# Gate, up and first-matrix products: low products of one half issued in turn with high products of the other half

## Chip, core and metric

The kernel runs on one core of a Trainium2 chip. The metric is device time in microseconds. A row of the profile can name several engines: PE is the matmul engine (TensorE), PEld its loads of the stationary operand, DVE the vector engine, ACT the scalar engine, POOL GpSimd, SP the engine that issues DMAs. TensorE's clock has two levels, 1.2 and 2.4 GHz; its granted share is 1.00 in the stretches shown here, which is 2.4 GHz.

## What is computed

Three transformer layers over 256 tokens of width 1024, in float32: a mixer of a bidirectional mLSTM and a spatial gating unit, a latent attention, and a chunked attention with a relative bias. Each has a feed-forward part behind it:

```python
x = x + jnp.square(jax.nn.relu(hf @ ffn_w1[layer])) @ ffn_w2[layer]      # layers 0 and 1, 1024 -> 4096 -> 1024
x = x + rms_norm_2(swiglu(h, w_gate, w_up, w_down), g_post_ffn)          # last layer, 1024 -> 2816 -> 1024
def swiglu(h, w_gate, w_up, w_down):
    return (jax.nn.silu(h @ w_gate) * (h @ w_up)) @ w_down
```

The products whose order is changed are `hf @ ffn_w1` (the first matrix of a feed-forward part), `h @ w_gate` and `h @ w_up`.

## The kernel before

Every weight comes from memory in pieces of 128 partitions by 2048 numbers (1 MB), in a ring of three slots. ScalarE rounds a piece to the matmul's reduced float32 (`w_hi`), and VectorE makes the rest, `w_lo = raw - w_hi`. The activations are split in the same way, into `h_hi` and `h_lo`, which lie side by side in `h_both`. A product is then a sum of three terms, high x high, high x low and low x high. The fourth is left out.

A piece of a first matrix has 256 output columns, in two halves of 128 (f = 0 and 1), and eight blocks of 128 input rows (k = 0 to 7). The function `stationary_both` (L2083) works one such piece. Half f has a PSUM bank of its own, `b + f`, with 512 columns of float32.

- A *high* product (L2090) has the block of `w_hi` as the stationary operand and streams 512 columns of `h_both`, that is `h_hi` and `h_lo` of the 256 tokens. The high x high terms end in columns 0 to 255 of the bank and the high x low terms in columns 256 to 511.
- A *low* product (L2096) has the block of `w_lo` as the stationary operand, streams the 256 columns of `h_hi` and adds to columns 0 to 255 of the same bank.

Each half needs eight highs and eight lows. Each of the 32 matmuls of a call has its own stationary operand. The order before is: eight highs of half 0, eight highs of half 1, eight lows of half 0, eight lows of half 1. When the last low has ended, `piece_used` is raised. DVE waits for it and adds the two 256-column parts of both banks in one reduction (L1608 in the first two feed-forward parts, L1925 and the one of `glu_mul` in the last). ScalarE waits for it before it writes the slot of the ring again.

Ahead of a call, PE waits with `split` until the `w_lo` of the piece is ready, and for the reduction that last read the two banks (`hid_in`, `gate_scaled` or `mul_out`).

The call stands in two loops. In `ffn` (L2423), which runs for two layers, the first piece has a function of its own, and each of the 15 further chunks is one call, followed by `out_piece` (L2176), the second matrix of the chunk before: 24 matmuls of 512 columns (L1984, L1985, L1986 in turn). In the last stage `gate_up` (L2855) makes one call for the gate and one for the up piece of each of ten chunks, and `out_piece` follows. Its very last call passes `half_done`: there half 0 is finished first (highs, lows) and then half 1, so that VectorE can begin with half 0.

Three other places are of use in reading the trace. `stationary_half` (L2070) does one half at a time, eight highs (L2076) and eight lows (L2079), in the projection of queries and keys of the last layer. `latent_in` (L2469) streams 384 and 288 columns in turn into two banks, and its low terms (L2048) alternate singly between the two sizes. `turn_x` (L2000) transposes blocks of 128 x 128 (L2005).

Of the kernel before, what the change touches and what calls it, by code (L numbers as in the profile page):

```python
# [34 lines left out]
P = 128  # L35
D = 1024
KB = D // P
S = 256
# [97 lines left out]
def build(nc, d, out):  # L136

    ctx = ExitStack()
    with ctx:
        def sb(name, shape, dt=F32):  # L140
            return ctx.enter_context(nc.sbuf_tensor(name, shape, dt))

        def sem(name):
            return ctx.enter_context(nc.semaphore(name))
# [9 lines left out]
        h_both = sb("h_both", [P, KB, 2, S], F32R)  # L154
        h_hi, h_lo = h_both[:, :, 0, :], h_both[:, :, 1, :]
# [144 lines left out]
        piece_used = sem("piece_used")  # L300
# [152 lines left out]
        def part(t, n, a):  # L453

            w = width(n)
            return t[:, n % RING, 0:w].rearrange("p (a b) -> p a b", a=a)
# [26 lines left out]
        def bank(b, n=1):  # L483
            return psum[:, b:b + n, :].rearrange("p b c -> p (b c)")
# [1496 lines left out]
        def _(pe):  # L1981
            def product(dst, stat, mov, first, last, shared=False):

                pe.matmul(dst, stat[0], mov[0], start=first, stop=False, skip_group_check=shared)  # L1984
                pe.matmul(dst, stat[0], mov[1], start=False, stop=False, skip_group_check=shared)  # L1985
                return pe.matmul(dst, stat[1], mov[0], start=False, stop=last, skip_group_check=shared)  # L1986

            def h_block(k, tb=None, t=None):
                if tb is None:
                    return h_hi[:, k, :], h_lo[:, k, :]  # L1990
                if t == T_2MIX:
                    return [mix_part(t, k // 2, a, b)[:, k % 2, tb * P:(tb + 1) * P]
                            for a, b in ((h_hi, g_hi), (h_lo, g_lo))]
                return h_hi[:, k, tb * P:(tb + 1) * P], h_lo[:, k, tb * P:(tb + 1) * P]
# [88 lines left out]
            def stationary_both(slot, b, half_done=None):  # L2083


                wh = w_hi[:, slot, :].rearrange("p (k c) -> p k c", k=KB)
                wl = w_lo[:, slot, :].rearrange("p (k c) -> p k c", k=KB)
                def high(f):
                    for k in range(KB):
                        pe.matmul(bank(b + f), wh[:, k, f * P:(f + 1) * P],  # L2090
                                  h_both[:, k, :, :].rearrange("p u s -> p (u s)"),
                                  start=k == 0, stop=False, skip_group_check=True)

                def low(f):
                    for k in range(KB):
                        ins = pe.matmul(bank(b + f)[:, 0:S], wl[:, k, f * P:(f + 1) * P], h_hi[:, k, :],  # L2096
                                        start=False, stop=k == KB - 1, skip_group_check=True)
                    return ins

                high(0)  # L2100
                if half_done is not None:
                    low(0).then_inc(half_done, 1)
                    high(1)
                else:
                    high(1)
                    low(0)
                low(1).then_inc(piece_used, 1)

            def stationary_seam(slot, t, b, x_at):

# [179 lines left out]
            for k in range(KB):  # L2290
                ins = product(bank(7)[0:3 * QUAD + A_H, 0:S],
                              (gw_hi[:, k, 0:3 * QUAD + A_H], gw_lo[:, k, 0:3 * QUAD + A_H]), h_block(k),
                              k == 0, k == KB - 1)
# [10 lines left out]
            wh = w_hi[:, 1, :].rearrange("p (k c) -> p k c", k=KB)  # L2304
            wl = w_lo[:, 1, :].rearrange("p (k c) -> p k c", k=KB)
            pe.wait_ge(hi_half, 2)
            for f in range(2):
                for k in range(KB):
                    at = bank(QK_ORDER[1])[:, f * S:(f + 1) * S]
                    pe.matmul(at, wh[:, k, f * P:(f + 1) * P], h_hi[:, k, :], start=f == 0 and k == 0, stop=False,  # L2310
                              skip_group_check=True)
                    pe.matmul(at, wh[:, k, f * P:(f + 1) * P], h_lo[:, k, :], start=False, stop=False,
                              skip_group_check=True)
# [3 lines left out]
            for f in range(2):  # L2317
                for k in range(KB):
                    ins = pe.matmul(bank(QK_ORDER[1])[:, f * S:(f + 1) * S], wl[:, k, f * P:(f + 1) * P], h_hi[:, k, :],
                                    start=False, stop=k == KB - 1, skip_group_check=True)  # L2320
# [10 lines left out]
            for q, rows in enumerate((a_row, mt_row)):  # L2331
                for tb in range(TB):
                    at = (2 * q + tb) * ROWS
                    ins = pe.transpose(bank(6)[:, at:at + ROWS], rows[0:ROWS, tb * P:(tb + 1) * P],
                                       ident[0:ROWS, 0:ROWS])
# [87 lines left out]
            def ffn(first, hb, t, x_at, x_next):  # L2423
                split(first)
                stationary_seam(first % RING, t, 0, x_at)

                def chunk(c, j, i):

                    n = first + 1 + 2 * j
                    split(n + 12 * i)  # L2430
                    if not (isinstance(c, int) and c == 0):
                        pe.wait_ge(hid_in, hb + c)
                    stationary_both(n % RING, hidden_banks(j + 1))
                    split(n + 1 + 12 * i)
                    pe.wait_ge(g_lo_ready, hb + c + 1)
                    out_piece(hidden_of(j % 3), (n + 1) % RING, isinstance(c, int) and c == 0)

                def hidden_of(r):
                    return lambda k, tb: (g_hi[:, r, k * S + tb * P:k * S + (tb + 1) * P],
                                          g_lo[:, r, k * S + tb * P:k * S + (tb + 1) * P])  # L2440

                for j in range(3):
                    chunk(j, j, 0)
                with pe.Fori(0, (FC - 4) // 6) as i:
                    for j in range(3, 9):
                        chunk(6 * i + j, j, i)
                n = first + 2 * FC - 1
                split(n)
                pe.wait_ge(g_lo_ready, hb + FC)
                out_seam(hidden_of((FC - 1) % 3), n % RING, x_next)  # L2450
# [55 lines left out]
            for j in range(3):  # L2506
                n = P_UQ + j
                split(n)
                wh, wl = part(w_hi, n, 3), part(w_lo, n, 3)
                if j:  # L2510
                    pe.wait_ge(latent_read, j)
                for tb in range(TB):
                    if j == 1 and tb == 1:
# [4 lines left out]
                        for t in range(TB):  # L2518
                            ins = pe.transpose(psum[0:C_QK, 4, t * P:(t + 1) * P], krr[:, t, :], ident[:, :])
                        ins.then_inc(krr_turned, 1)  # L2520
                    for k in range(3):
                        if j == 0 and tb == 0 and k == 2:
                            turn_latent(1, 0, 3)
                        if j == 0 and k < 2:
                            latent_wait(2 * tb + k)
                        ins = product(bank(UQ_BANKS[j] + tb), h_block(k, tb), (wh[:, k, :], wl[:, k, :]),
                                      k == 0, k == 2)
# [18 lines left out]
            def c_values(j, tb):  # L2546

                wh, wl = part(w_hi, P_UKV + j, 2), part(w_lo, P_UKV + j, 2)
                for k in range(2):
                    ins = product(bank((0, 4)[j] + tb), h_block(3 + k, tb), (wh[:, k, 512:], wl[:, k, 512:]),  # L2550
                                  k == 0, k == 1)
                return ins
# [3 lines left out]
            for j in range(2):  # L2556
                n = P_UKV + j
                split(n)
                wh, wl = part(w_hi, n, 2), part(w_lo, n, 2)
                pe.wait_ge(evac_q, 2 + j)  # L2560

                for pair in range(4):
                    hs = slice(pair * P, (pair + 1) * P)
                    for k in range(2):
                        ins = product(bank((6, 2)[j], 2)[:, pair * S:(pair + 1) * S],
                                      (wh[:, k, hs], wl[:, k, hs]), h_block(3 + k), k == 0, k == 1)
# [7 lines left out]
                if j == 0:  # L2574
                    for tb in range(TB):
                        ins = c_values(0, tb)
# [278 lines left out]
            def gate_up(c, r, n0, i):  # L2855
                split(n0 + 6 * i)
                if not (isinstance(c, int) and c == 1):
                    pe.wait_ge(gate_scaled, c)
                stationary_both(n0 % RING, 4)
                split(n0 + 1 + 6 * i)  # L2860
                pe.wait_ge(mul_out, hb + c)
                stationary_both((n0 + 1) % RING, 6, up_half if isinstance(c, int) and c == GC - 1 else None)
# [53 lines left out]
```

## Time and profile before

| | us |
|---|---|
| median of three runs (873.94 to 874.26) | 874.14 |
| the profiled execution | 874.67 |
| its span, from the first to the last instruction | 872.9 |
| PE busy | 864.1 (99%) |
| PEld busy | 739.8 (85%) |
| DVE busy | 622.4 (71%) |
| ACT busy | 452.9 (52%) |

The profile is of one execution. Busy times of PE overlap, since a matmul begins before the one ahead of it has ended, so the mean duration of a matmul is longer than the distance from one to the next. The distances stand in the chain of waits, which shares the time out among the instructions that followed each other, and in the starts of a timeline. Both are given to 0.01 us. A run of the same line is merged into one row with its count.

### The profile page before, as it was taken

The page shows a single profiled execution, that of the slowest core. Times are in us where ns is not written, and L with a number is a line of the kernel's source. Part 1 is how long each engine was busy: PE and PEld are TensorE (multiplying, and loading weights), DVE is VectorE, ACT ScalarE, POOL GpSimd, SP SyncE. Part 2 cuts the span into 40 slices and gives each one's busy share as a digit, 9 for nine tenths or more (in the row PEclk, how much of TensorE's full clock was granted, in tenths as well). Part 3 has the DMA queues.
Part 4 walks back from the last instruction along what each step waited for, and adds up shares of the span by engine and source line. Part 5 has one row for each costly group of instructions (what it writes and reads, how often), then busy time and mean ns, then how long its engine had stood idle before and what let it go on. Part 6 is the DMA issues. An engine that isn't in the chain of part 4 may idle for free.

```text
span 872.9 us, 12188 instructions
## 1 busy us (share of the span) xinstructions
PE 864.1 (99%) x4714; PEld 739.8 (85%) x4714; DVE 622.4 (71%) x783; ACT 452.9 (52%) x619; POOL 80.9 (9%) x115
## 2 busy tenths in 40 slices
PE   9999999999999999999999999999999999999997
PEld 8988888888888988778888888888877888888886
DVE  6899877766666678857666666667775876676675
ACT  5697554433434578745343444465775844434432
POOL 3484110000000020011000000020000200000000
PEclk9999999999999999999999999999999999999999
DMA  9665356565555362376655555556442456555541
GB/s 303 213 215 193 112 179 219 169 212 192 187 189 193 116 191 86 106 250 204 207 192 190 190 191 193 188 182 200 145 146 97 140 178 213 193 191 193 192 145 48
DMA packets 98393, 155.84 MB, mean 179 GB/s; under 512 B 4144, under 2 KB 73421, under 8 KB 98349
## 3 DMA queue, kind: packets, MB, share of 16 engines
q1 hardware_dynamic: 95644, 149.37, 51.0%
q0 software_dynamic: 1648, 5.80, 2.2%
q8 instruction: 29, 0.48, 0.2%
q10 hardware_dynamic: 1056, 0.07, 0.1%
q14 instruction: 16, 0.12, 0.0%
HBM read 153.62 MB, written 1.09 MB: 177 GB/s over the span
## 4 chain that ended last, share of the span: by engine, by line
PE 98%; DMA 1%; DVE 0%; ACT 0%; issue 0%; SPq 0%; DVEq 0%; POOLq 0%; POOL 0%; ACTq 0%
PE psum L2090 21%; PE psum L1984 16%; PE psum L1985 16%; PE psum L1986 16%; PE psum L2096 11%; PE psum L2076 4%; PE psum L2079 2%; PE psum L2591 1%; PE psum L2622 1%; PE psum L2005 1%; PE psum L2268 1%; PE psum L2604 1%; PE psum L2043 1%; PE psum L2048 1%; PE psum L2044 1%; PE psum L2702 1%
## 5 line engine op out<-in xcount | busy, mean ns | idle before, releaser
L1297 DVE TENSOR_TENSOR w_lo<-raw,w_hi 128x2048 fp32r<-128x2048 f32 (+3 forms) x116 | 259.6, 2247 | 79.9 <-ACT w_hi L793 39.1
L2090 PE MATMUL psum<-h_both,w_hi 128*128 128x512 f32 x800 | 190.0, 389 | 0.0
L2090 PEld LDWEIGHTS psum<-h_both,w_hi 128*128 128x128 f32 x800 | 149.3, 188 | 30.4
L775 ACT ACTIVATE w_hi<-raw 128x2048 fp32r<-128x2048 f32 (+2 forms) x71 | 129.6, 1838 | 36.6 <-PE psum L1986 23.6
L1984 PE MATMUL psum<-w_hi,g_hi 128*128 128x512 f32 x368 | 144.6, 393 | 0.0
L1985 PE MATMUL psum<-w_lo,g_hi 128*128 128x512 f32 x368 | 143.7, 390 | 0.0
L1986 PE MATMUL psum<-w_hi,g_lo 128*128 128x512 f32 x368 | 143.3, 389 | 0.0
L793 ACT ACTIVATE w_hi<-raw 128x2048 fp32r<-128x2048 f32 x66 | 125.7, 1911 | 23.9 <-PE psum L1986 23.9
L2096 PEld LDWEIGHTS psum<-h_both,w_lo 128*128 128x128 f32 x800 | 102.7, 191 | 4.0
L968 ACT ACTIVATE g_hi<-g_mul 128x512 fp32r<-128x512 f32 x32 | 20.3, 634 | 162.7 <-DVE g_mul L1612 162.7
L2096 PE MATMUL psum<-h_both,w_lo 128*128 128x256 f32 x800 | 103.9, 283 | 0.0
L1984 PE MATMUL psum<-w_hi,h_both 128*128 128x512 f32 (+1 forms) x202 | 82.0, 406 | 0.0
L1986 PEld LDWEIGHTS psum<-w_hi,g_lo 128*128 128x128 f32 x368 | 69.1, 188 | 14.7
L1984 PEld LDWEIGHTS psum<-w_hi,g_hi 128*128 128x128 f32 x368 | 69.3, 188 | 13.5 <-issue 0.5
L1985 PEld LDWEIGHTS psum<-w_lo,g_hi 128*128 128x128 f32 x368 | 69.3, 188 | 12.5
L645 POOL TENSOR_SCALAR msq<-ssq 128x1 f32<-128x1 f32 (+1 forms) x22 | 17.7, 803 | 669.5 <-ACT junk L819 650.2
L1986 PE MATMUL psum<-w_hi,h_both 128*128 128x512 f32 (+1 forms) x202 | 77.9, 385 | 0.0
L1985 PE MATMUL psum<-w_lo,h_both 128*128 128x512 f32 (+1 forms) x202 | 77.7, 385 | 0.0
L1608 DVE TENSOR_REDUCE g_act<-psum 128x512 f32<-128x1024 f32 x30 | 36.7, 1224 | 31.6 <-PE psum L2096 31.6
L1312 DVE TENSOR_TENSOR w_lo<-raw,w_hi 128x2048 fp32r<-128x2048 f32 x18 | 40.7, 2289 | 21.7 <-ACT w_hi L793 21.7
L1984 PEld LDWEIGHTS psum<-w_hi,h_both 128*128 128x128 f32 x202 | 38.0, 188 | 7.8 <-DVE h_both L1651 0.6
L1986 PEld LDWEIGHTS psum<-w_hi,h_both 128*128 128x128 f32 x202 | 37.9, 188 | 7.6
(312 smaller groups left out, 1098.5 us busy)
## 6 DMA issues: line engine op xcount, KB each, us to landing
raw<-in_ffn_w SPq DMA_DIRECT2D x64, 1024.0 KB, 5.3
raw<-in_w_qkv SPq DMA_DIRECT2D x12, 1024.0 KB, 5.1
raw<-in_ab_w_in SPq DMA_DIRECT2D x11, 1024.0 KB, 6.5
raw<-in_w_gate SPq DMA_DIRECT2D x11, 1024.0 KB, 5.3
raw<-in_w_up SPq DMA_DIRECT2D x11, 1024.0 KB, 5.4
raw<-in_w_down SPq DMA_DIRECT2D x11, 1024.0 KB, 5.7
raw<-in_ab_w_out SPq DMA_DIRECT2D x4, 1024.0 KB, 4.9
raw<-in_c_w_out SPq DMA_DIRECT2D x4, 1024.0 KB, 6.5
```

The costliest lines, as they stand in the source:

```text
L775: ins = act.activation(dst, src, ACT.Copy)
L793: act.activation(w_hi[:, slot, :], raw[:, slot, :], ACT.Copy).then_inc(hi_ready, 1)
L968: act.activation(g_hi[:, r, :], g_mul[:, r, :], ACT.Copy).then_inc(g_hi_ready, 1)
L1297: ins = dve.tensor_tensor(dst, src, high, ALU.subtract)
L1312: dve.tensor_tensor(w_lo[:, slot, :], raw[:, slot, :], w_hi[:, slot, :], ALU.subtract)\
L1608: ins = dve.tensor_reduce(g_act[:, r, :].rearrange("p (f t) -> p f t", f=2), sums_of(hidden_banks(c)), AX.X, ALU.add)
L1984: pe.matmul(dst, stat[0], mov[0], start=first, stop=False, skip_group_check=shared)
L1985: pe.matmul(dst, stat[0], mov[1], start=False, stop=False, skip_group_check=shared)
L1986: return pe.matmul(dst, stat[1], mov[0], start=False, stop=last, skip_group_check=shared)
L2076: pe.matmul(bank(b), wh[:, k, cs], h_both[:, k, :, :].rearrange("p u s -> p (u s)"), start=k == 0, stop=False, skip_group_check=True)
L2090: pe.matmul(bank(b + f), wh[:, k, f * P:(f + 1) * P], h_both[:, k, :, :].rearrange("p u s -> p (u s)"), start=k == 0, stop=False, skip_gro ...
L2096: ins = pe.matmul(bank(b + f)[:, 0:S], wl[:, k, f * P:(f + 1) * P], h_hi[:, k, :], start=False, stop=k == KB - 1, skip_group_check=True)
```

## The change

The two inner functions now issue one product each, with k as an argument, and the loops over k stand at the place of the call. In the order without `half_done`, the eight highs of half 1 and the eight lows of half 0 are issued in turn: high(1, 0), low(0, 0), high(1, 1), low(0, 1), and so on. The two write to different banks. The eight highs of half 0 ahead of them and the eight lows of half 1 behind them are unchanged, and so is the order with `half_done`. No instruction is added or left out, each bank still gets its highs ahead of its lows, and `piece_used` is raised by the same instruction.

```diff
-                def high(f):
+                def high(f, k):
+                    pe.matmul(bank(b + f), wh[:, k, f * P:(f + 1) * P],
+                              h_both[:, k, :, :].rearrange("p u s -> p (u s)"),
+                              start=k == 0, stop=False, skip_group_check=True)
+
+                def low(f, k):
+                    return pe.matmul(bank(b + f)[:, 0:S], wl[:, k, f * P:(f + 1) * P], h_hi[:, k, :],
+                                     start=False, stop=k == KB - 1, skip_group_check=True)
+
+                for k in range(KB):
+                    high(0, k)
+                if half_done is not None:
                     for k in range(KB):
-                        pe.matmul(bank(b + f), wh[:, k, f * P:(f + 1) * P],
-                                  h_both[:, k, :, :].rearrange("p u s -> p (u s)"),
-                                  start=k == 0, stop=False, skip_group_check=True)
-
-                def low(f):
+                        ins = low(0, k)
+                    ins.then_inc(half_done, 1)
                     for k in range(KB):
-                        ins = pe.matmul(bank(b + f)[:, 0:S], wl[:, k, f * P:(f + 1) * P], h_hi[:, k, :],
-                                        start=False, stop=k == KB - 1, skip_group_check=True)
-                    return ins
-
-                high(0)
-                if half_done is not None:
-                    low(0).then_inc(half_done, 1)
-                    high(1)
+                        high(1, k)
                 else:
-                    high(1)
-                    low(0)
-                low(1).then_inc(piece_used, 1)
+                    for k in range(KB):
+                        high(1, k)
+                        low(0, k)
+                for k in range(KB):
+                    ins = low(1, k)
+                ins.then_inc(piece_used, 1)
```

## Rows read from the trace of the kernel before

**Rows 1.** Page: busy us (share of span) and instructions; chain by engine and line.
```profile
PE 864.1 (99%) x4714; PEld 739.8 (85%) x4714; DVE 622.4 (71%) x783; ACT 452.9 (52%) x619; POOL 80.9 (9%) x115
PE 98%; DMA 1%; DVE 0%; ACT 0%; issue 0%; SPq 0%; DVEq 0%; POOLq 0%; POOL 0%; ACTq 0%
PE psum L2090 21%; PE psum L1984 16%; PE psum L1985 16%; PE psum L1986 16%; PE psum L2096 11%; PE psum L2076 4%; PE psum L2079 2%; PE psum L2591 1%; PE psum L2622 1%; PE psum L2005 1%; PE psum L2268 1%; PE psum L2604 1%; PE psum L2043 1%; PE psum L2048 1%; PE psum L2044 1%; PE psum L2702 1%
```

**Rows 2.** Waits of PE, whole span: us in total, times, longest us.
```profile
PE psum L2234 <- POOL ones L628: 1.0, 1, 1.0
...
PE psum L2604 <- DVE arena L1738: 0.2, 1, 0.2
```

**Rows 3.** Chain of waits, one chunk: start us, us, what.
```profile
409.95 3.63 PE psum L2090 x16
413.58 1.91 PE psum L2096 x16
415.50 0.23 PE psum L1984
```

**Rows 4.** Page, groups: busy us, mean ns of one, idle us before them.
```profile
L2090 PEld LDWEIGHTS psum<-h_both,w_hi 128*128 128x128 f32 x800 | 149.3, 188 | 30.4
L2096 PEld LDWEIGHTS psum<-h_both,w_lo 128*128 128x128 f32 x800 | 102.7, 191 | 4.0
```

**Rows 5.** Waits in the chunk from 409.79 to 420.80 us, VectorE for the last low.
```profile
DVE g_act L1608 <- PE psum L2096: 0.4, 1, 0.4
```

**Rows 6.** Timeline of PE: first and third low of a run, two places (start us first).
```profile
413.42 0.28 PE L2096 MATMUL psum<-h_both,w_lo 128*128 128x256 f32 x1
413.65 0.52 PE L2096 MATMUL psum<-h_both,w_lo 128*128 128x256 f32 x3
126.39 0.28 PE L2096 MATMUL psum<-h_both,w_lo 128*128 128x256 f32 x1
126.63 0.40 PE L2096 MATMUL psum<-h_both,w_lo 128*128 128x256 f32 x2
```

**Rows 7.** Timeline of PE, the 512-column matmuls right behind the lows.
```profile
415.33 0.40 PE L1984 MATMUL psum<-w_hi,g_hi 128*128 128x512 f32 x1
...
415.80 0.39 PE L1986 MATMUL psum<-w_hi,g_lo 128*128 128x512 f32 x1
```

**Rows 8.** Chain of waits, the projection with runs of eight (`stationary_half`).
```profile
593.54 1.81 PE psum L2076 x8
595.36 0.95 PE psum L2079 x8
596.31 1.84 PE psum L2076 x8
```

**Rows 9.** Chain of waits, first half of the last call (`half_done` order).
```profile
850.52 1.84 PE psum L2090 x8
852.36 0.95 PE psum L2096 x8
```

**Rows 10.** Chain of waits, alternating low terms of `latent_in`, first and last of four.
```profile
295.63 0.62 PE psum L2048 x4
...
...
303.00 0.61 PE psum L2048 x4
```

**Rows 11.** Timeline of PE: second high of a run, first low, next high (projection).
```profile
608.60 0.39 PE L2076 MATMUL psum<-h_both,w_hi 128*128 128x512 f32 x1
...
610.22 0.28 PE L2079 MATMUL psum<-h_both,w_lo 128*128 128x256 f32 x1
...
611.16 0.40 PE L2076 MATMUL psum<-h_both,w_hi 128*128 128x512 f32 x1
```

**Rows 12.** Chain of waits, a run of 128-column transposes.
```profile
297.18 0.87 PE psum L2005 x8
```

## The prediction

> **What bounds the kernel now.** I read the page's busy shares and its chain first, then TensorE's waits, then one chunk of the chain, then the starts of single matmuls. The reader is to see that PE is busy 99% of the span and makes up 98% of the chain that ended last, and that the changed function alone, L2090 (high products) and L2096 (low products), holds 21% and 11% of it [rows 1]. PE waits for others five times in the whole span, for 1.0 us at most, and never on L2090 or L2096 [rows 2]. So nothing around this function is late: its cost is the spacing of its own matmuls, and a shorter or longer spacing goes into the end one for one.
>
> Busy times are no spacing, since matmuls and loads overlap (a load of 191 ns in each low [rows 4]). The spacing is in the chain: 16 highs take 3.63 us, 0.2269 each; 16 lows 1.91 us, 0.1194 each; the 24 matmuls behind them go by 0.23 [rows 3]. One high and one low therefore cost 0.3463 us today, and a call of the function 5.54 us. Twice the columns cost 0.1075 us more, 0.42 ns per column, and at either size some 12 ns stand on top of what the columns explain. The question is what an alternation does to these 12 ns.
>
> **How much is reordered.** L2090 and L2096 have 800 weight loads each, one per matmul [rows 4], at 16 per call 50 calls: 15 in each of two FFNs, 20 in the last stage (gate and up of ten pieces). The one call with `half_done` keeps its order. That leaves 49 calls, in each of which eight highs of the second half and eight lows of the first now alternate: 392 pairs. The first eight highs and last eight lows stay runs.
>
> **What the edit adds and removes.** No instruction, weight load, column or byte: both orders issue the same 32 matmuls. No wait is added or moved: `split` and the wait for the banks still stand ahead of the first high, and `piece_used` is still on the last low, which DVE's reduction awaits (0.4 us of idle time in one chunk [rows 5]). That reduction reads both banks at once, so finishing bank b one order or another frees nothing. DMA issues, ScalarE and VectorE are triggered by the same instruction as before. Each of these edits costs nothing because the event that others see is the last matmul of the call; if the call gets longer by x, they all come x later and PE, which has no waits here, is late by x and no more. What is left is 392 pairs times the difference to 0.3463 us.
>
> **The price of a pair.** The trace holds no 512-column matmul alternating singly with a 256-column one, so I bound it.
>
> *Below:* the first low behind highs is the cheapest low. The first two lows of a run take 0.23 us in one place and 0.24 in another [rows 6]; less 0.119 for the second, the first takes 0.111 to 0.121. If every low were that first one and the highs kept 0.2269, a pair would cost 0.338 to 0.348, up to 8 ns less: 392 x 8.3 ns = 3.3 us saved.
>
> *Above:* a high behind lows is dearer. The first two 512-column matmuls behind the lows stand 0.47 us apart, 0.235 each [rows 7]. The same shows in the chain of the projection where runs of eight alternate: eight highs behind another stage's 512-column matmuls take 1.81 us, and behind lows 1.84 [rows 8]; the last call, in the `half_done` order, takes twice 1.84 + 0.95, 5.58 us against 5.54 [rows 9]. So changing from low to high and back did not pay in any row: 0.03 us per change. At 0.235 + 0.1194 a pair would cost 0.354, 8.1 ns more: 3.2 us lost.
>
> *Between:* two nearest rows. The latent projection's L2048 alternates singly a 384-column and a 288-column matmul, into two banks: four stretches of 0.62, 0.31, 0.31 and 0.61 us (four, two, two and four matmuls), that is six pairs in 1.85, 0.3083 each (the first and the last of the four stand in [rows 10]). By the straight line through 0.1194 at 256 and 0.2269 at 512 columns, 288 is 0.1328 and 384 is 0.1732, together 0.3060: alternation costs 2.3 ns a pair over runs. The second: behind a late start the projection runs in an unsettled spacing, seven highs from 608.60 to 610.22, 0.2314 each, and eight lows from 610.22 to 611.16, 0.1175 each [rows 11]; a pair of these is 0.3489, 2.6 ns over. Both near cases agree; I take 2.5 ns, since it is the single alternation of unequal sizes that the new order makes, and keep both ends. 392 x 2.5 ns = +0.98 us.
>
> *Different banks:* 16 highs that change bank once cost 3.63, twice the 1.81 of eight in one bank [rows 3, 8], so back-to-back accumulation into one bank shows no stall that another bank could remove. I count nothing for it. The Trainium skill (Perfetto Trace Analysis, Matmul Optimizations) advises using all eight PSUM banks for parallelism, which speaks for the edit; by the rows just named it is worth nothing where every matmul already accumulates at full spacing.
>
> **The sum.** The profiled execution took 874.67 us, a span of 872.9 and 1.8 around it; it becomes 875.65. It lies 0.53 above the median of 874.14, to which the same 0.98 is added: 875.1 us.
>
> **Rivals.**
>
> *A, the weight load is hidden (faster).* In the lows the weight-load rows have nearly no gap (4.0 us idle over 800), in the highs 30.4 us [rows 4]. If the lows' 12 ns over their columns are the wait for the next weights, a long matmul ahead of each low lets its load finish early, as for the first low of a run: a pair of 0.338 to 0.348, in the middle 0.340 to 0.341 with the first low at 0.114, 2.3 us saved, 871.8 us. Against it: every low is now followed by the load for a high, of the same 128 x 128, which must fit behind the low as before; the highs have the same 12 ns although their loads have time; and 128-column transposes, each with a load of its own, go by 0.109 (eight in 0.87) [rows 12], so loads as such can follow each other closer than the lows do. The Trainium skill (TensorE: Matmul & The Clock Gate, LDWEIGHTS) gives a load as 128 columns over 1.2 GHz, 107 ns, and in its section on the back-to-back gap 109 ns for 256 columns; by an estimate from that page the lows would fall from 119 to 109 if nothing but the load held them, 4 us in all, and no row here shows a low at 109. In the page's own terms load and stream of a low are tied, so it gives order little to win.
>
> *B, each change is paid in full (slower).* A high behind lows is slow for its first few issues and settles only in a run of highs [rows 7, 8]; singly alternated highs never settle. Place: the eight highs of the second half. Price: 8 ns on each while the lows stay at 0.1194, 3.2 us, 877.3 us. It decides from 4.5 ns a pair on (1.75 us). For it: every change from lows to highs in the rows costs. Against: L2048 pays 2.3, because the small one behind a large one gets some back.
>
> *C, order is free.* The 12 ns belong to each matmul whatever its neighbour; the pair stays at 0.3463 and the time at 874.1. The straight line, with equal excess at 256 and 512, speaks for it; the 1.84 against 1.81 speaks against it. "The change doesn't do what it says" is part of it: there is no stall between products of one bank to be removed.
>
> *D, the unsettled spacing outlives the function* and takes the 24 matmuls behind it (4.5 ns each, 0.2314 less 0.2269, behind 40 calls 4.3 us: about 878.5 with nothing else). Against it, the eight lows that still end the call: behind the unsettled run, the projection's next highs start from a run of eight lows as all others do.
>
> **Chances.** Forecast (1 to 4 ns a pair lost) 0.45; C 0.17; A 0.16; B 0.19; D 0.03. What a measurement can tell from no change is about 0.2%, 1.75 us, 4.5 ns a pair. Faster by more: most of A, 0.14. Slower by more: B, D and the upper edge of the forecast, 0.25. Within: 0.61. The range takes most of A and of B: 871.4 to 877.5.
>
> **What would show it.** In the chain, a chunk's 5.54 us for 16 highs and 16 lows becomes 5.56; the first eight highs stay at 1.81, the last eight lows at 0.95, and eight alternating pairs take 2.79 (A: 2.73, B: 2.84, C: 2.77). The starts of the single matmuls, which then have different lines, show highs at 0.23 and lows at 0.12. PE's waits stay as they are and DVE's idle time unchanged. I am wrong if pairs fall outside 0.343 to 0.351, or if the next 24 matmuls are no longer 0.23 apart.

## The result and the profile after

| | before | changed |
|---|---|---|
| median, us (13 runs each) | 874.54 | 876.54 |
| lowest to highest | 873.94 to 875.09 | 876.08 to 877.05 |
| profiled span | 872.9 | 874.9 |

The changed kernel is slower: ratio 1.0024, 95% interval 1.0016 to 1.0032, 2.0 us. That is inside the range and on the forecast side, at twice the forecast loss, and just beyond the 0.2% that the prediction set as the border. The median before is now 874.54 instead of 874.14, from more runs.

The page of the changed kernel, busy shares and the weight loads of the two groups of the function (columns as in [rows 1] and [rows 4]; L2089 is now the high product and L2094 the low):

```profile
PE 866.1 (99%) x4714; PEld 739.6 (85%) x4714; DVE 622.6 (71%) x783; ACT 452.5 (52%) x619; POOL 80.6 (9%) x115
...
L2089 PEld LDWEIGHTS psum<-h_both,w_hi 128*128 128x128 f32 x800 | 149.3, 188 | 32.7
...
L2094 PEld LDWEIGHTS psum<-h_both,w_lo 128*128 128x128 f32 x800 | 126.5, 189 | 4.1
```

PE's busy time grew by the same 2.0 us as the span. The counts are the same. The idle gaps ahead of the loads are 32.7 and 4.1 us, against 30.4 and 4.0. The low loads are busy for 126.5 us instead of 102.7 because loads of 190 ns that follow each other every 0.12 us overlap, and time in which two of them run counts once; next to highs they overlap each other less. The waits of PE are the same five as in [rows 2]. VectorE's wait for the last low in the chunk that [rows 5] shows is 0.5 us instead of 0.4. So no other engine shows a part in this.

The chain of waits of the changed kernel in the chunk that answers to [rows 3] (start us, us, what):

```profile
410.69 2.04 PE psum L2089 x9
412.73 0.12 PE psum L2094
412.85 0.23 PE psum L2089
413.08 0.12 PE psum L2094
413.20 0.24 PE psum L2089
...
415.20 1.08 PE psum L2094 x9
416.28 0.23 PE psum L1984
```

The first nine highs stand at 0.227 as before (2.04 / 9). From the first low at 412.73 to the run of lows at 415.20 there are seven pairs of a low and a high in 2.47 us, 0.3529 each, against 0.3463 in runs: 6.6 ns more. In these rows the low keeps its 0.12 and the high behind it takes 0.23 or 0.24, on average 0.233 where it took 0.227. How the price is shared between the two depends on what is read. From one start in the timeline to the next, averaged over the chunks, a high inside the alternation takes 0.236 and a low 0.116 to 0.117. In a run a high takes 0.2267, the first low 0.113 and the lows from the fourth on 0.120, so that 0.1194 is a mean of 16 with a cheap first one. The sum of a pair is firm: three pairs in the middle take 1.060 us, 0.3533 each, against 0.3467 for a settled high and a settled low. The call lasts 5.59 us (410.69 to 416.28), where it lasted 5.55 (409.95 to 415.50 in [rows 3]).

A more exact measure, used for every kernel below, is the distance from the first highs of one chunk to those of a later one. Before, the 13 chunks of the first feed-forward part (chain of waits):

```profile
133.94 3.63 PE psum L2090 x16
277.02 3.63 PE psum L2090 x16
```

After, in the same view:

```profile
134.10 2.04 PE psum L2089 x9
277.70 2.04 PE psum L2089 x9
```

That is 143.08 us against 143.60: a chunk of 11.006 became one of 11.046. With 0.040 us in each of 49 calls, the sum is 1.96 us, all of the measured 2.0. Each of the 392 pairs costs 5.0 ns net, less than the 6.6 inside the alternation. The starts, averaged over the 13 chunks, show where the rest goes. The call grows by 49 ns (5.539 to 5.588 us), and the first five 512-column matmuls behind it give 9 back (1.161 to 1.152 us); the 19 after them take 4.307 us in both.

### The profile page after: what moved, and what is told of

Same layout as the page of the kernel before. It is cut to its first block, busy times and chain, and to the rows that moved or that the text cites. A ratio compares the mean times of both kernels' runs of the same rounds, so it can differ in the third digit from the quotient of the medians.

```text
span 874.9 us, 12188 instructions
## 1 busy us (share of the span) xinstructions
PE 866.1 (99%) x4714; PEld 739.6 (85%) x4714; DVE 622.6 (71%) x783; ACT 452.5 (52%) x619; POOL 80.6 (9%) x115
## 4 chain that ended last, share of the span: by engine, by line
PE 98%; DMA 1%; DVE 0%; ACT 0%; issue 0%; SPq 0%; DVEq 0%; POOLq 0%; POOL 0%; ACTq 0%
PE psum L2089 21%; PE psum L1984 16%; PE psum L1986 15%; PE psum L1985 15%; PE psum L2094 11%; PE psum L2076 4%; PE psum L2079 2%; PE psum L2595 1%; PE psum L2626 1%; PE psum L2005 1%; PE psum L2608 1%; PE psum L2272 1%; PE psum L2043 1%; PE psum L2048 1%; PE psum L2044 1%; PE psum L2706 1%
## 5 line engine op out<-in xcount | busy, mean ns | idle before, releaser
L2089 PE MATMUL psum<-h_both,w_hi 128*128 128x512 f32 x800 | 233.0, 393 | 0.0
L2089 PEld LDWEIGHTS psum<-h_both,w_hi 128*128 128x128 f32 x800 | 149.3, 188 | 32.7
L2094 PE MATMUL psum<-h_both,w_lo 128*128 128x256 f32 x800 | 159.5, 282 | 0.0
L2094 PEld LDWEIGHTS psum<-h_both,w_lo 128*128 128x128 f32 x800 | 126.5, 189 | 4.1
```

The lines of the kernel that those rows point to most:

```text
L2089: pe.matmul(bank(b + f), wh[:, k, f * P:(f + 1) * P], h_both[:, k, :, :].rearrange("p u s -> p (u s)"), start=k == 0, stop=False, skip_gro ...
L2094: return pe.matmul(bank(b + f)[:, 0:S], wl[:, k, f * P:(f + 1) * P], h_hi[:, k, :], start=False, stop=k == KB - 1, skip_group_check=True)
```

## The experiments

### Is it the size or the bank?

The edits below are shortened and stand against the changed kernel; H is a high, L a low. Two things alternate in the changed kernel: the number of columns and the bank. Two kernels alternate one of them alone, and a third doubles the pairs and keeps the bank inside each half.

```diff
 # e1_one_bank: high and low of the same half in turn
+for k in range(KB): high(0, k)
+for k in range(KB): high(1, k); low(1, k)
+for k in range(KB): ins = low(0, k)
```

> The same single alternation of high and low products in 49 calls, but both in one bank: highs of half 0, then high and low of half 1 in turn, then the lows of half 0. Theory S (the price is that of alternating 512 and 256 columns, whatever the bank): as the changed kernel, 2.0 us over before, a chunk of the feed-forward part 11.05 us against 11.01, high 0.23 to 0.24 and low 0.12 in turn. Theory K (the price is that of changing the bank at each matmul): as before, 874.5 us within 0.3, chunk 11.01.

```diff
 # e2_banks_in_turn: equal sizes in turn, another bank at each matmul
+for k in range(KB): high(0, k); high(1, k)
+for k in range(KB): low(0, k); ins = low(1, k)
```

> The bank changes at every matmul, the size does not: high 0 and high 1 in turn, then low 0 and low 1 in turn, in 49 calls. Theory S: nothing, 16 highs in 3.63 us, 16 lows in 1.91 us, 874.5 us. Theory K: twice as many changes of bank as the changed kernel, so 2 to 4 us slower, 876.5 to 878.5.

```diff
 # e3_all_pairs: every high is followed by a low of its own half
+for k in range(KB): high(0, k); low(0, k)
+for k in range(KB): high(1, k); ins = low(1, k)
```

> All 16 highs and lows of a call alternate singly, each half in its own bank. Theory S: twice the pairs of the changed kernel at 0.353 each, 16 x 6.7 ns more per call, less the some 20 ns that the run of lows at the end of a call costs today: 80 to 105 ns in 49 calls, 4 to 5 us over before, 878.5 to 879.7. Theory K: no change of bank inside a half, so 874.5.

| kernel | median, us | before in the same runs | ratio, 95% interval | chunk, us |
|---|---|---|---|---|
| e1_one_bank | 876.59 | 874.68 | 1.0021 (1.0012 to 1.0030) | 11.046 |
| e2_banks_in_turn | 874.50 | 874.68 | 0.9996 (0.9987 to 1.0005) | 11.007 |
| e3_all_pairs | 879.57 | 874.68 | 1.0052 (1.0039 to 1.0066) | 11.107 |

The chunks are from the chain of waits, first and last of 13. e1_one_bank:

```profile
134.33 2.04 PE psum L2089 x9
277.93 2.04 PE psum L2089 x9
```

e2_banks_in_turn, the same view, with the sixteen lows of one chunk as the last line:

```profile
133.92 3.63 PE psum L2089 x16
277.01 3.63 PE psum L2089 x16
413.57 1.91 PE psum L2094 x16
```

e3_all_pairs, the same view:

```profile
133.32 0.23 PE psum L2089
277.71 0.23 PE psum L2089
```

The reader is to see 143.60 for one bank, exactly as in the changed kernel, and 143.09 for banks in turn, as before (143.08), with 3.63 and 1.91 as in [rows 3]. The bank is worth nothing in either direction; the turn of sizes makes up all of it. With all 16 pairs the chunk grows by 0.101 us; 49 times that is 4.9 us, and 4.9 was measured. Theory S held in all three.

### Is it unequal sizes, the other weights, or a load that is only just in time?

In the changed kernel `w_hi` and `w_lo` also take turns as the stationary operand, and a short low may leave little time for the next load. Three kernels change how many columns a low product streams. In each, the feed-forward calls have runs of 16 and 16, and the gate and up calls alternate singly as in the changed kernel, so that one profile has both.

```diff
-pe.matmul(bank(b + f)[:, 0:S], wl[:, k, f * P:(f + 1) * P], h_hi[:, k, :], ...)
+pe.matmul(bank(b + f)[:, 0:N], wl[:, k, f * P:(f + 1) * P], h_both[k] columns 0 to N, ...)   # N = 512, 128, 384
```

> The low products stream 512 columns instead of 256 (they add the low x low term, which the kernel before leaves out). Feed-forward calls keep runs of 16 and 16, gate and up calls alternate singly as in the changed kernel. Theory S (unequal column counts are what costs): equal spacing of 0.227 in both, a single alternation 0.453 a pair, a gate or up call 7.25 us. Theory O (it is the turn between w_hi and w_lo as stationary operand that costs): 7 ns a pair on top, 0.460, a call 7.31 us. Whole kernel 85 us slower by the added columns either way.

> The low products stream only 128 columns (the low x high term of tokens 128 to 255 is left out); feed-forward calls in runs, gate and up calls alternating singly. Theory L (a low waits for the weight load that follows it, whatever it streams): a low in a run stays at 0.12 and the kernel at 875 us. Theory C (columns plus a fixed excess): a low in a run takes 0.066 and the kernel is some 40 us faster. Between them, 0.109 as the transposes of 128 columns. In the single alternation, theory S expects at least the 7 ns a pair of 512 and 256 over what the runs take.

> The low products stream 384 columns (with half of the low x low term added); feed-forward calls in runs, gate and up calls alternating singly. If the price of the single alternation comes from the load behind a short low being only just in time, it is gone at 384 columns: a pair 0.400, equal to runs. If it comes from unequal counts as such, 2 to 7 ns a pair stay. In runs a low takes 0.174.

One execution each: 958.8, 869.9 and 919.9 us, against 874.3 for the kernel before. These differ in work; what counts are the spacings in the chain of waits, and those repeat from chunk to chunk within 0.01 us. e6_low_128, lows in a run, then the alternation:

```profile
159.21 1.74 PE psum L2094 x16
744.10 0.06 PE psum L2094
744.16 0.28 PE psum L2089
...
746.49 0.62 PE psum L2094 x6
```

The same view, the first highs of the chunks that are compared (the second feed-forward part, 13 chunks in runs, then gate and up, 8 chunks alternating):

```profile
408.36 3.63 PE psum L2089 x16
550.24 3.63 PE psum L2089 x16
709.29 2.04 PE psum L2089 x9
840.38 2.04 PE psum L2089 x9
```

e7_low_384, lows in a run, then the alternation:

```profile
150.15 2.80 PE psum L2094 x16
786.36 0.17 PE psum L2094
...
789.20 1.56 PE psum L2094 x9
```

The same view, first highs as above (12 chunks in runs, 8 alternating):

```profile
424.14 3.63 PE psum L2089 x16
567.02 3.63 PE psum L2089 x16
741.00 2.04 PE psum L2089 x9
888.31 2.04 PE psum L2089 x9
```

Inside the alternation:

| columns of the low | low, mean of a run of 16 | pair in runs | pair alternating singly | difference, ns |
|---|---|---|---|---|
| 512 | 0.227 | 0.4537 | 0.4533 (6 in 2.72) | 0 |
| 384 | 0.1750 | 0.4019 | 0.4057 (7 in 2.84) | 3.8 |
| 256 (changed kernel) | 0.1194 | 0.3463 | 0.3529 (7 in 2.47) | 6.6 |
| 128 | 0.1088 | 0.3357 | 0.3414 (7 in 2.39) | 5.7 |

These differences mislead, since the mean of a run holds what a change of size does to its first lows: at 384 columns they take up to 0.185 and then settle at 0.173, at 128 the first takes 0.058 and the others 0.112 (starts, averaged). The distance between chunks holds all of it. A feed-forward chunk is a call and 24 matmuls of 0.2267 us, a gate and up chunk two calls and 24 matmuls, so in runs the second would take twice the first less 5.44. For the kernel before that gives 16.572, and 16.574 is measured (8 chunks, 712.39 to 844.98).

| columns of the low | feed-forward chunk, in runs | gate and up, in runs | gate and up, alternating | a call of 8 pairs, ns |
|---|---|---|---|---|
| 512 | 12.693 (12, 436.79 to 589.11) | 19.946 | 19.946 (8, 766.20 to 925.77) | 0 |
| 384 | 11.907 (12) | 18.373 | 18.414 (8) | 20 |
| 256 (changed kernel) | 11.006 (13) | 16.574 | 16.653 (8, 713.80 to 847.02) | 40 |
| 128 | 10.914 (13) | 16.388 | 16.386 (8) | 0, within 1 |

With equal sizes the turn between `w_hi` and `w_lo` as stationary operand costs nothing, so theory O falls. At 384 columns 20 ns a call stay, 2.5 a pair, although a low of 0.173 leaves more time for the next load than the 0.112 at which 128-column lows, each with a load, follow each other. So a load that is only just in time isn't all of the price. At 128 columns the alternation costs nothing net, where theory S expected at least 7 ns a pair. Unequal sizes as such are therefore not the whole answer either: the price is there for 256 and 384 columns against 512, and not for 128.

e6 also bears on what holds a low. With half the columns a settled low falls only from 0.120 to 0.112, near the 0.109 of the transposes in [rows 12], so at 128 columns it is no longer the columns that set the spacing. Theories L (0.12) and C (0.066) are both wrong for 128 columns, and the value between them, which the expectation named, is nearly right. The settled 0.2267, 0.1733 and 0.1200 of 512, 384 and 256 columns lie on one line: each is its columns at 2.4 GHz plus 13.3 ns.

### How much does a coarser turn cost?

```diff
 # e4_groups: group = 2 in the feed-forward calls, 4 in gate and up; highs of half 0 ahead, lows of half 1 behind, as before
+for k0 in range(0, KB, group):
+    for k in range(k0, k0 + group): high(1, k)
+    for k in range(k0, k0 + group): low(0, k)
```

> The order of the changed kernel in coarser steps: two highs, two lows in turn in the feed-forward calls, four and four in the calls of gate and up. Theory F (a fixed price per change from low to high, 6.7 ns): 27 ns in a feed-forward call and 13 ns in a gate or up call, so chunks of 11.03 (before 11.01, changed 11.05) and some 16.59 (before 16.57, changed 16.66). Theory R (each high in the first six behind lows pays what it pays in a long run, 7, 8, 2, 5, 4 ns, and the first low gives back 7): 30 ns per call in both, chunks of 11.03 and 16.62. Together 1 to 1.5 us over before.

Measured: 874.80 us against 874.68, ratio 1.0000 (0.9991 to 1.0009). Both theories had 1 to 1.5 us over. The chain of waits of e4_groups, feed-forward chunks (first and last of 13), then gate and up chunks (first and last of 8):

```profile
134.21 2.27 PE psum L2089 x10
277.30 2.27 PE psum L2089 x10
712.69 2.72 PE psum L2089 x12
845.39 2.72 PE psum L2089 x12
```

The feed-forward chunk is 143.09 / 13 = 11.007 us, not above before. The gate and up chunk is 132.70 / 8 = 16.588, where before has 16.574 and the changed kernel 16.653, so 7 ns for each of its two calls, less than either theory had. A fixed price per change from low to high doesn't exist: with more changes, the steps of two cost less than the steps of four.

```diff
 # e8_orders: three orders, H the next high, L the next low
+first feed-forward part:  (H H L L) x 8
+second:                   H x 8, (H H L) x 4, L x 12
+gate and up:              H x 8, (H L L) x 4, H x 4, L x 8
```

> Three orders of the same products. First feed-forward part: two highs, two lows in turn over all 32. Second: eight highs, four times two highs and one low, twelve lows. Gate and up: eight highs, four times one high and two lows, four highs, eight lows. Theory P (a high that stands alone between lows is what pays, 10 ns each; two together pay nothing net, as the steps of two showed): chunk of the first part 11.01 us as before or less, of the second 11.01, and a gate and up chunk 4 x 2 x 10 ns over 16.57, 16.65. Theory F (a fixed price per change): all three above before, the first most.

One execution: 875.53 us against 874.31. The chain of waits of e8_orders, first and last chunks of the first part (13), the second (13), and gate and up (8):

```profile
133.77 0.45 PE psum L2089 x2
276.94 0.45 PE psum L2089 x2
409.92 2.27 PE psum L2089 x10
553.27 2.27 PE psum L2089 x10
712.70 2.04 PE psum L2089 x9
845.82 2.04 PE psum L2089 x9
```

```diff
 # e9_threes
+first feed-forward part:  H x 8, (H H H L L L) x 2, H H L L, L x 8
+second:                   H x 9, L, H x 7, L x 15
+gate and up:              H x 16 (gate), H x 16 (up), L x 16 (gate), L x 16 (up)
```

> First feed-forward part: eight highs, then three highs and three lows twice, two and two, eight lows. Second: one lone low after nine highs, then seven highs and fifteen lows. Gate and up: all highs of both pieces first, then all their lows, one change from lows to highs less per chunk. Theory A (alone or not: only matmuls standing alone between the other size pay): first part 11.01 us a chunk as before, second 11.01 to 11.02 (one lone low, 5 to 7 ns), gate and up 16.55 against 16.57. Theory E (odd steps pay, even steps do not): first part 11.03 to 11.05. Whole kernel within 0.3 us of before by A, 0.5 us over by E.

The chain of waits of e9_threes, first and last chunks of the first and the second part:

```profile
133.27 2.49 PE psum L2089 x11
276.62 2.49 PE psum L2089 x11
409.62 2.04 PE psum L2089 x9
552.97 2.04 PE psum L2089 x9
```

All orders, as the cost of one call over the runs of 16 and 16 (chunk less 11.006, or half of the chunk less 16.574). A turn is a change from lows to highs; the one at the end of the call, into the next highs or 512-column matmuls, is counted.

| order of highs and lows | turns | ns a call |
|---|---|---|
| runs of 16 and 16 (before) | 1 | 0 |
| steps of one, 8 pairs (the change; e1) | 8 | 40 |
| steps of one, 16 pairs (e3) | 16 | 101 |
| steps of two, 8 pairs (e4, e10) | 4 | 0 |
| steps of two, 16 pairs (e8) | 8 | 7 |
| steps of three, three and two (e9) | 3 | 21 |
| steps of four, 8 pairs (e4) | 2 | 7 |
| three lone lows, two highs between them (e8) | 4 | 21 |
| three lone highs, two lows between them (e8) | 5 | 33 |
| one lone low (e9) | 2 | 21 |

In the second and third order of e8 the fourth lone one joins the run next to it. Theory P, that only lone highs pay, falls with the lone lows (11.027 where it had 11.01). Theory F falls there too, since the first part, with the most changes, is the cheapest. Theory A falls with the steps of three and with the one lone low, 21 ns where 5 to 7 were expected. Theory E has the steps of three right (11.027), but the one lone low shows that the count of changes is not it either.

Two things can be read from the table. First, a chunk is known within 1 ns, a call of gate and up within half of that, and so far every entry is a whole number of steps of 6.7 ns: 6, 15, 0, 1, 3, 1, 3, 5 and 3. Second, runs are not free of the cost. The 40 settled highs and 512-column matmuls (0.2267) and 16 settled lows (0.1200) of a chunk make 10.987 us, and the kernel before takes 11.006 to 11.007, three such steps more, for its single turn: the five 512-column matmuls behind the lows take 1.161 us instead of 1.133, and the first low returns 7 ns. The one lone low makes a second turn far from the first and costs the same three steps again. Turns close together cost less each: eight at steps of one 60 ns in all, four at steps of two 20, as much as one. Why steps of two share so well and steps of one so badly stays open.

### An order that should have been better

The gate and up part of e9_threes has one change from lows to highs less per chunk, and by the spacings it should have saved 0.02 us in each. The kernel took 910.1 us instead, ratio 1.0399 (1.0384 to 1.0413), and all of the loss is in that stage. The waits of PE in e9_threes (us, times, longest):

```profile
PE psum L2116 <- DVE w_lo L1312: 15.3, 6, 2.6
PE psum L2116 <- DVE w_lo L1297: 5.0, 2, 2.6
```

The timeline of its ScalarE around one of them (idle before and releaser in brackets):

```profile
748.86 0.63 ACT L1236 ACTIVATE g_act<-g_act 128x512 f32<-128x512 f32 x1 [10.09 <-DVE g_act L1927]
749.40 1.90 ACT L793 ACTIVATE w_hi<-raw 128x2048 fp32r<-128x2048 f32 x1
```

The window of its PE in the highs behind one such wait (busy us, twice, with instructions; granted clock; DMA share; GB/s):

```profile
739.50:744.80 5.30, 5.30 (x17) 0.68 0.81 269
```

The gate's last low, and with it `piece_used`, came only after all highs of the up piece. ScalarE stood 10.09 us for the gate's activation (at most 5.6 us in the kernel before), and the rounding of a later piece of weights is queued behind it. PE then waited for `w_lo`, 20.3 us in eight places. Behind the wait of 2.56 us that ended at 739.43, the granted clock was 0.68 on average, so that part of these highs ran at the lower level of 1.2 GHz, and the sixteen took 5.49 us in the chain instead of 3.63. The kernel lost some 35 us, against 2.0 by the change itself. The waits make up 20.3 of them; that the lower clock makes up the other 15 is likely but not added up here. The prediction's sentence that each of its edits costs nothing holds only while the event that others see stays in place; here it moved by a run of 16 highs. What the missing turn saves by itself can't be seen under this loss.

### The change in steps of two

```diff
 # e10_twos, all 49 calls
+H x 8, (H H L L) x 4, L x 8
```

> The changed kernel with steps of two in place of steps of one in all 49 calls: eight highs, then two highs and two lows four times, eight lows; the same 392 pairs alternate, in the same two banks. Theory A: the whole loss of 2.0 us goes, 874.5 us, chunks of 11.01 and 16.57. Theory F (a price per change): half of the loss stays, 875.5.

Measured: 874.65 us against 874.63, ratio 0.9998 (0.9989 to 1.0007). The chain of waits of e10_twos, feed-forward chunks (13), then gate and up (8):

```profile
133.80 2.27 PE psum L2089 x10
276.89 2.27 PE psum L2089 x10
712.32 2.27 PE psum L2089 x10
844.90 2.27 PE psum L2089 x10
```

11.007 and 16.573 us: before has 11.006 and 16.574. The same products alternate in the same two banks, and the whole loss is gone. No order that was tried beats the kernel before.

## Why the prediction came out as it did

**The time** came inside the range and on the side that was forecast, with 2.0 us where 0.98 were forecast. By the prediction's own sign of being wrong the price failed, though: pairs were to stay within 0.343 to 0.351 and take 0.353 inside the alternation, and 5.0 ns net is more than the forecast's 1 to 4. The range held because it took in most of rivals A and B as well, so that it held says little for the price.

**What bounds the kernel** was right. PE has the same five waits, and 49 calls of 0.040 us give the whole difference. That the edit frees or delays nothing for others held too; e9_threes shows what it costs when it doesn't hold.

**No gain from different banks** was right, and shown apart: e2 alternates banks at every matmul for nothing, e1 pays the full price in one bank.

**The price of a pair** is the step that was mis-sized: 2.5 ns taken, 5.0 measured. Both near rows were of another kind than the new order. L2048 alternates 384 and 288 columns in stretches of two pairs at most and pays 2.3; e7 with 512 and 384, the same ratio, pays 2.5 net. So that row was read rightly for its sizes, but 512 and 256 pay twice as much, and 512 and 128 nothing: the price doesn't carry over from one pair of sizes to another. The unsettled rows [rows 11] were runs of seven and eight, and runs say little of single steps, as the table of orders shows, so their agreement at 2.6 was no confirmation. For the inside of the alternation the upper end was nearly right: 0.235 for a high behind lows [rows 7] plus 0.1194, 0.354 a pair, and 0.353 was measured.

**Rival B** is about as near to what happened as the forecast. For it, the highs inside the alternation don't settle and are dearer, 0.233 for 0.227 in the chain, and the net price of 5.0 ns lies past the 4.5 from which B was said to decide. Against it, 8 ns a pair were 6.7 inside the alternation and 5.0 over a call, since by the starts the lows return some ns and so do the matmuls behind the call. B had a chance of 0.19 and slower beyond 0.2% had 0.25, which was too little. Its cause as I put it, that highs settle only in a run of highs, doesn't decide the price: in steps of two highs don't settle either (0.231 to 0.236 by the starts), and nothing is lost net, because lows return it.

**Rival A** fell. A pair became dearer, not cheaper, and the idle gaps of the loads stayed near what they were, 4.1 and 32.7 us. By e6 the floor under a low with a load is 0.112, so at most 0.008 of a settled low's 0.120 could be bought by an earlier load. The Trainium skill (TensorE: Matmul & The Clock Gate, Back-to-back issue gap) gives 109 ns for 256 columns, for a matmul counted by itself. In the runs of lows shown here it isn't reached: settled lows take 120 ns, those of the shortest run 117.5 each [rows 11].

**Rival C** fell with e10 beside the changed kernel: order is not free, it is free only in some steps. **Rival D** did not happen: by the starts the first three matmuls after the function take 0.235, 0.2325 and 0.231 and the rest 0.2267, so they settle sooner than before.

## What to carry to other kernels

Where TensorE is the bound and matmuls of unequal column counts can be ordered freely, keep equal ones together, or look at the distance between two chunks for each order. Here single alternation of 512 and 256 columns cost 5 ns a pair net, steps of two nothing, and single alternation of 512 and 128 nothing. Compare whole chunks and not single spacings: a change of size moves time between neighbours. A price for a new order is read from rows with the same two sizes and the same length of run; where there are none, only the bounds are worth giving. An order that saves nanoseconds on the bound engine must leave the last product of each piece where it is, since here ScalarE took up the next rounding only behind the work that waits for that product.

## What was not expected

- Steps of two of 512 and 256 columns cost nothing (0 ns a call), steps of one 40, steps of three 21, steps of four 7. No theory here explains this row of numbers.
- One lone low among highs costs a call 21 ns, as much as three of them.
- All orders cost whole steps of 6.7 ns a call, within what the rows show.
- Alternating with 128-column lows, the low takes 0.06 and the high behind it 0.28: what the short one saves in the chain stands in the next one's time. Over a whole chunk this alternation costs nothing, where 256 columns pay 40 ns a call.
